# Gate and branch projections as seven half-size block products per column pair, gates ahead of branches

## The chip, the cores and the metric

The kernel is one inference step of a one-layer hybrid encoder and runs on one core of a Trainium2 chip. The metric is the device time of one launch in microseconds. Below, PE is TensorE (the matrix engine), DVE is VectorE, ACT is ScalarE, POOL is GpSimd and SP is the sync engine, whose queue issues the weight loads.

## The reference, cut to what matters

512 prompt tokens and 64 sample tokens (T = 576 together) pass through a mixer, a memory attention and a mixture of experts. The change is in the end of the mixer, which merges two branches under sigmoid gates:

```python
h = rmsnorm(x, norm_mix)                              # 576 x 1024
z, xbc_raw, dt_raw, q, k, v, gl_ssm, gl_sb = split_cols(h @ w_in)
...                                                   # y: the state-space scan, times d_skip and so on
y_ssm = rmsnorm(y * jax.nn.silu(z), ssm_norm) @ w_ssm_br            # K = 1024
y_sb = stick_breaking(qh, k_all, v_all, off).reshape(bsz, L, SB_INNER) @ w_sb_br   # K = 512
merged = jax.nn.sigmoid(gl_ssm) * y_ssm + jax.nn.sigmoid(gl_sb) * y_sb
return x + merged @ w_out, new_conv, h_last, kh, vh
```

Of this, three projections of 1024 x 1024 are touched: the two gate logits (`gl_ssm` and `gl_sb`, from `h`) and `y_ssm`. `y_sb`, with half their depth, is computed as before but at another time.

## The kernel before, in words

All activations lie transposed: 128 partitions of channels, 8 slices k, T = 576 token columns. A product is made exact to float32 by splitting each operand into a rounded high part and a low rest, and taking three matmuls, high x high, high x low and low x high (`passes`). `tproj` does this for one block of 128 output channels: two halves of 288 tokens, 8 slices, 3 matmuls, that is 48 matmuls of 128x288 (24 where the depth is 512). A weight tile comes in by SP (`load`) to one of four `RAW` buffers; ACT casts it to the high part (`split_high`), DVE subtracts to leave the rest in place (`split_low`).

The order of all work is written out by hand: each engine has its own program, and semaphores tie them. An engine executes strictly in its order, so what stands behind a waiting instruction waits too. The stages around the change are:

- the z projection (`z_rows(0..7)` on PE, `z_out` on ACT), with eight blocks of 128 channels;
- the state-space scan, ten steps v of `ssd_first` and `ssd_second` on PE, with exponentials on ACT, products on DVE (`xdt` and the lines behind it) and one product a step on POOL;
- the mixing stage, `for c in range(KD)` on each engine: for each of eight channel blocks c, PE makes both gate projections (48 matmuls each), the `w_ssm_br` projection (48) and the `w_sb_br` projection (24); ACT takes the sigmoids, DVE multiplies and adds (`mg_ready`), ACT and DVE split the result into `MGH` and `MG`. Weights of a block are two tiles, W_M + 2c and W_M + 2c + 1. Between the scan and the first branch product stand the squares of `ZS`, their sum over channels by PE (`squares_sum`) and `token_scale`, which is the rmsnorm factor `RB`;
- the output projection (`out_part`, `rproj`), which starts with the first seven slices of `MG`.

## Time and profile before

| | |
|---|---|
| median of 3 runs | 1194.85 us (1194.77 to 1195.83) |
| span of the profiled execution | 1192.3 us, so 2.55 us of the median lie around the span |
| PE, DVE, ACT, POOL busy | 1140.7, 715.9, 564.9, 121.0 us |
| mixing stage on PE | from 394.14 to 574.94 us, 180.8 us |

A busy PE counts each matmul until its modelled end, and the matmuls overlap; what one costs is therefore read from the starts of the first and the last of a run of them. DVE, ACT and POOL times are of the instructions themselves.

### The profile page before, as it was taken

Reading aid. Unit: us, or ns where it says so; the run is one execution under the profiler, and the core shown is the slowest. Engines: PE = TensorE matmul, PEld = TensorE weight load, DVE = VectorE, ACT = ScalarE, POOL = GpSimd, SP = SyncE. Lnnn points to the kernel's source line nnn. Section 1 sums busy time; section 2 is a strip of 40 time slices with the busy share of each in tenths; the row PEclk is TensorE's granted clock in tenths of the full one; section 3 lists DMA queues with packets and bytes.
Section 4 is the critical chain, followed back from the end, with each engine's and each line's share of the span. In section 5 each row is a group of like instructions: output and inputs, shape, how many; then the busy total and the mean of one; then the engine's idle time right before and its main releaser. Section 6 shows DMA issues by size and latency. Waiting matters only on the chain.

```text
span 1192.3 us, 18490 instructions
## 1 busy us (share of the span) xinstructions
PE 1140.7 (96%) x7908; PEld 1033.2 (87%) x7908; DVE 715.9 (60%) x850; ACT 564.9 (47%) x709; POOL 121.0 (10%) x147
## 2 busy tenths in 40 slices
PE   6999899999999999999999999999899999999994
PEld 6988789999986999999999999989667878778873
DVE  6325664866268642332535633534589998889884
ACT  6334553334386622222315523312176867778763
POOL 2003340000044000000000000000001000000050
PEclk9999989999999999999999999999799999999997
DMA  9421110323210232332526602201899999999995
GB/s 296 143 74 36 36 41 1 107 71 103 67 28 1 71 89 63 97 89 72 186 71 230 215 15 72 72 1 58 306 343 393 420 410 378 394 400 385 374 258 148
DMA packets 95038, 197.27 MB, mean 165 GB/s; under 512 B 4208, under 2 KB 71960, under 8 KB 82664
## 3 DMA queue, kind: packets, MB, share of 16 engines
q1 hardware_dynamic: 87328, 169.88, 40.5%
q0 software_dynamic: 5440, 18.76, 5.4%
q10 hardware_dynamic: 2184, 7.39, 1.5%
q8 instruction: 65, 1.06, 0.4%
q14 instruction: 21, 0.17, 0.1%
HBM read 178.41 MB, written 17.61 MB: 164 GB/s over the span
## 4 chain that ended last, share of the span: by engine, by line
PE 74%; DVE 10%; ACT 9%; issue 4%; DMA 2%; ACTq 0%; POOL 0%; SPq 0%; DVEq 0%; POOLq 0%
PE ps L2248 45%; PE ps L1032 6%; ACT buf_r L959 4%; DVE buf_r L966 4%; PE ps L1042 3%; PE ps L2688 2%; PE ps L2704 2%; PE ps L2369 1%; ACT buf_r L461 1%; DVE buf_r L1181 1%; PE ps L2398 1%; PE ps L2399 1%; PE ps L1016 1%; PE ps L2377 1%; ACT buf L1160 1%
## 5 line engine op out<-in xcount | busy, mean ns | idle before, releaser
L2248 PE MATMUL ps<-buf_r,buf_r 128*128 128x288 f32 (+1 forms) x4488 | 590.9, 292 | 7.3 <-ACT buf L1675 2.6
L2248 PEld LDWEIGHTS ps<-buf_r,buf_r 128*128 128x128 f32 x4488 | 578.8, 189 | 11.6 <-issue 6.7
L966 DVE TENSOR_TENSOR buf_r<-buf,buf_r 128x2048 fp32r<-128x2048 f32 x92 | 205.0, 2283 | 0.0
L1032 PE MATMUL ps<-buf_r,buf_r 128*128 128x512 f32 x720 | 174.5, 397 | 0.0
L959 ACT CAST buf_r<-buf 128x2048 fp32r<-128x2048 f32 x92 | 170.9, 1909 | 0.0
L446 DVE TENSOR_TENSOR buf_r<-buf,buf_r 128x2048 fp32r<-128x2048 f32 (+2 forms) x49 | 107.5, 2195 | 101.2 <-ACT buf_r L440 101.2
L1032 PEld LDWEIGHTS ps<-buf_r,buf_r 128*128 128x128 f32 x720 | 133.2, 188 | 29.7 <-issue 0.5
L440 ACT CAST buf_r<-buf 128x2048 fp32r<-128x2048 f32 (+2 forms) x53 | 96.7, 1824 | 99.6 <-PE ps L2248 55.1
L1042 PE MATMUL ps<-buf_r,buf_r 128*128 128x512 f32 x384 | 89.8, 389 | 0.5 <-DVE buf_r L1209 0.5
L1042 PEld LDWEIGHTS ps<-buf_r,buf_r 128*128 128x128 f32 x384 | 72.0, 188 | 15.8 <-DVE buf_r L1209 0.9
L461 ACT CAST buf_r<-ps 128x512 fp32r<-128x512 f32 (+2 forms) x41 | 30.0, 731 | 75.6 <-PE ps L1016 63.2
L558 ACT ACTIVATE buf<-buf 128x1024 f32<-128x1024 f32 (+1 forms) x22 | 23.2, 1056 | 43.0 <-DVE buf L2169 18.6
L1232 POOL DMA_INDIRECT buf<-hn_rows,buf x16 | 17.2, 1074 | 233.6 <-DVE buf L626 133.6
L1903 DVE COPY buf<-ps 128x1280 f32<-128x1280 f32 x10 | 14.9, 1490 | 36.1 <-PE ps L2369 29.7
L1565 POOL TENSOR_TENSOR buf<-buf,buf 128x1024 f32<-128x1024 f32 x10 | 27.8, 2783 | 58.1 <-ACT buf L1752 58.1
L1682 ACT ACTIVATE buf<-buf 128x1280 f32<-128x1280 f32 x10 | 12.7, 1275 | 41.4 <-POOL buf L1529 30.2
L1974 DVE SCALAR_TENSOR_TENSOR buf<-buf,buf,buf 128x579 f32<-128x579 f32 x36 | 29.6, 822 | 1.3
L1181 DVE TENSOR_TENSOR buf_r<-ps,buf_r 128x1024 fp32r<-128x1024 f32 x15 | 18.4, 1225 | 18.5 <-ACT buf_r L461 18.5
L461 ACT CAST buf_r<-buf 128x1024 fp32r<-128x1024 f32 (+4 forms) x20 | 19.0, 949 | 21.8 <-DVE buf L2105 11.6
L1817 ACT ACTIVATE buf<-ps 128x288 f32<-128x288 f32 x16 | 6.6, 411 | 46.5 <-PE ps L2248 46.5
L2398 PE MATMUL ps<-buf_r,buf_r 128*128 128x256 f32 (+1 forms) x78 | 26.8, 359 | 1.2 <-DVE buf_r L1913 1.2
L1529 POOL TENSOR_SCALAR_AFFINE_SELECT buf<-buf 128x128 f32<-128x128 f32 x32 | 20.2, 668 | 75.8 <-DVE buf L1903 75.8
(339 smaller groups left out, 1291.3 us busy)
## 6 DMA issues: line engine op xcount, KB each, us to landing
buf<-in_w_gate_e SPq DMA_DIRECT2D x32, 1024.0 KB, 8.1
buf<-in_w_up_e SPq DMA_DIRECT2D x32, 1024.0 KB, 7.6
buf<-in_w_down_e SPq DMA_DIRECT2D x32, 1024.0 KB, 7.4
buf<-in_w_in SPq DMA_DIRECT2D x16, 1024.0 KB, 5.6
buf<-in_w_in SPq DMA_DIRECT2D x17, 512.0 KB, 4.5
buf<-in_w_mem_kv SPq DMA_DIRECT2D x8, 1024.0 KB, 5.8
y_rows<-buf ACTq DMA_DIRECT2D x14, 512.0 KB, 8.4
buf<-in_x_prompt SPq DMA_DIRECT2D x8, 512.0 KB, 5.5
```

The costliest lines, as they stand in the source:

```text
L440: nc.scalar.copy(w_hi(n), tile_view(RAW[n % NRAW], n)).then_inc(wh_ready, 1)
L446: nc.vector.tensor_tensor(r32(raw), raw, w_hi(n), ALU.subtract).then_inc(wl_ready, 1)
L461: nc.scalar.copy(r32(hi), src).then_inc(ah_ready, 1)
L959: nc.scalar.copy(e_hi(t), e_raw(t)).then_inc(wh_ready, 1)
L966: nc.vector.tensor_tensor(e_lo(t), e_raw(t), e_hi(t), ALU.subtract).then_inc(wl_ready, 1)
L1032: last = nc.tensor.matmul(bank(b), r32(a[:, k, :]), w[:, i, :], start=(k == 0 and j == 0), stop=(k == KD - 1 and j == 2))
L1042: last = nc.tensor.matmul(bank(5 + c), r32(a[:, k, :]), w[:, i, 512 * c:512 * (c + 1)], start=(k == 0 and j == 0), stop=(k == 3 and j == 2))
L1181: nc.vector.tensor_tensor(r32(GT[e % 2]), bank(0, 2).rearrange("p (c n) -> p c n", c=KD), r32(GTH[e % 2]), ALU.subtract).then_inc(al_ready, 1)
L1565: nc.gpsimd.tensor_tensor(CE[v % 2], CE[v % 2], bc(XC[:, 10 + g, c * P:(c + 1) * P].unsqueeze(1), [P, 8, P]), ALU.mult).then_inc(ce_ready, 1)
L1974: o = nc.vector.scalar_tensor_tensor(out=cv[:, 0:579], in0=xr[:, j:j + 579], scalar=CW[:, j, i:i + 1], in1=cv[:, 0:579], op0=ALU.mult, op1 ...
L2248: last = nc.tensor.matmul(out, a, b, start=(k == 0 and j == 0), stop=(k == len(parts) - 1 and j == 2))
L2398: nc.tensor.matmul(out, m, high[:, oj:oj + nj], start=(j == kc), stop=False)
```

## The change

The eight blocks of each gate, and the eight of `w_ssm_br`, are now taken as column pairs i: i = 0 to 7 is block i of both gates, i = 8 to 11 is blocks 2(i - 8) and 2(i - 8) + 1 of `w_ssm_br`. For a pair, the weight is a 2 x 2 matrix of blocks (two column blocks by two halves of the depth), the activations are 2 x 2 as well (two halves of the depth by two halves of 288 tokens), and the eight block products are replaced by seven (the Winograd form of Strassen's scheme). That needs four sums of weight blocks for each pair (`sums`, in `S_RAW`), their high and low parts (`high_s`, `low_s`), four sums of activation blocks (T1 to T4) with high and low parts, made once for `h` and once for the scaled `ZS`, and copies and additions between the products (`u1_out`, `u2_out`, `u3_out` on ACT, `c11`, `c12`, `c22` on DVE). `MG` and `MGH` now hold the gates until the branch products meet them. `w_sb_br` is loaded in four chunks of two channel blocks into a buffer of its own (`SBR`, high part `SBH_`). The sums of squares and the scaling of the first gate by `RB` go to POOL. `MT` (memory tokens) is stored to a DRAM tensor early and loaded back behind the stage, since its place is needed.

The core of the diff:

```diff
+        m_tiles = []
         for c in range(0, D, P):
-            tiles.append(([(0, cols(w_in, C_GS + c, P)), (8, cols(w_in, C_GB + c, P))], P))
-            tiles.append(([(0, cols(I["w_ssm_br"][0], c, P)), (8, cols(I["w_sb_br"][0], c, P))], P))
+            m_tiles.append((cols(w_in, C_GS + c, P), cols(w_in, C_GB + c, P)))
+        for c in range(0, D, 2 * P):
+            m_tiles.append((cols(I["w_ssm_br"][0], c, P), cols(I["w_ssm_br"][0], c + P, P)))
...
+            return a[:, 4 * j:4 * j + 4, k * H2:(k + 1) * H2]
...
+        A_RAW = [RAW[i].rearrange("p (s n) -> p s n", n=P) for i in (1, 0)]
+        S_RAW = [RAW[i].rearrange("p (s n) -> p s n", n=P) for i in (2, 3)]
...
+            def load_m(i):
...
+                    sp.wait_ge(m_psum, m_at["p2", i - 2])
+                for j, src in enumerate(m_tiles[i]):
+                    sp.dma_start(A_RAW[i % 2][:, 8 * j:8 * j + 8, :], src).then_inc(ring_loaded[1 - i % 2], 16)
+            def load_sb(p):
+                if p == 0:
+                    sp.wait_ge(m_psum, m_at["p3", KD - 1])
+                else:
+                    sp.wait_ge(m_psum, m_at["sb", 2 * p - 1])
+                sp.dma_start(SBR, cols(I["w_sb_br"][0], 2 * P * p, 2 * P)).then_inc(mix_loaded, 16)
...
+            t_pool_step(1, T3, T3, r32(part(HT, 1, 1)), ALU.add)
+            t_pool_step(2, T3, T3, r32(part(HT, 0, 1)), ALU.subtract)
+            pool.wait_ge(t_made, 5)
+            t_pool_step(3, T4, r32(part(HTH, 1, 0)), T2, ALU.subtract)
+            t_pool_step(4, T4, T4, r32(part(HT, 1, 0)), ALU.add)
...
-            for c in range(KD):
...
-                nc.scalar.activation(halves(GS[c % 2]), pair(0), ACT.Sigmoid).then_inc(gs_ready, 1)
...
-                nc.scalar.activation(halves(GB[c % 2]), pair(2), ACT.Sigmoid).then_inc(gb_ready, 1)
-                split_high(act, W_M + 2 * c + 2)
...
+            def u3_out(i):
...
+                nc.scalar.copy(U3, x_sum(i)).then_inc(part_ready, 1)
...
+                act_high(MGH[:, c, :], MG[:, c, :])
+            def sb_high(p):
+                act.wait_ge(mix_loaded, 16 * (p + 1))
+                if p:
+                    act.wait_ge(m_psum, m_at["sb", 2 * p - 1])
+                nc.scalar.copy(r32(SBH_), SBR).then_inc(b_high, 1)
...
+            for i in range(NM):
+                u1_out(i)
+                if 1 <= i <= KD:
+                    gate_b_first(i - 1)
...
+                if i + 1 < NM:
+                    high_a(i + 1)
...
+                u2_out(i)
+                if i + 1 < NM:
+                    high_s(i + 1)
+                if 1 <= i <= KD:
...
+                    act_high(YSBTH, YSBT)
+                if i >= KD:
+                    sb_high(i - KD)
+                if i > KD:
+                    merged_high(2 * (i - KD - 1))
+                u3_out(i)
+                if i > KD:
+                    merged_high(2 * (i - KD - 1) + 1)
...
+                nc.vector.tensor_tensor(out, a, b, op).then_inc(t_made, 1)
...
+            dve.wait_ge(mt_stored, 16)
+            t_sum(0, T1, r32(part(HTH, 0, 1)), r32(part(HTH, 0, 0)), ALU.subtract)
+            t_sum(1, T1, T1, r32(part(HT, 0, 1)), ALU.add)
+            t_sum(2, T1, T1, r32(part(HT, 0, 0)), ALU.subtract)
+            t_sum(3, T2, r32(part(HTH, 1, 1)), T1, ALU.subtract)
+            t_sum(4, T2, T2, r32(part(HT, 1, 1)), ALU.add)
...
-            split_low(dve, W_M)
+            def sums(i):
...
+                nc.vector.tensor_tensor(o[:, 0:4], a[:, 8:12], a[:, 12:16], ALU.add).then_inc(sums_made, 1)
+                nc.vector.tensor_tensor(o[:, 8:12], a[:, 0:4], a[:, 8:12], ALU.subtract)
+                dve.wait_ge(sums_made, 3 * i + 1)
+                nc.vector.tensor_tensor(o[:, 4:8], o[:, 0:4], a[:, 0:4], ALU.subtract).then_inc(sums_made, 1)
+                dve.wait_ge(sums_made, 3 * i + 2)
+                nc.vector.tensor_tensor(o[:, 12:16], a[:, 4:8], o[:, 4:8], ALU.subtract).then_inc(sums_made, 1)
...
+            def low_a(i):
...
+                nc.vector.tensor_tensor(r32(A_LOW[q]), A_RAW[q][:, 12:16], r32(A_HIGH[q][:, 8:12]), ALU.subtract)
+                nc.vector.tensor_tensor(r32(A_RAW[q][:, 0:8]), A_RAW[q][:, 0:8], r32(A_HIGH[q][:, 0:8]),
+                                        ALU.subtract).then_inc(m_low, 1)
+            def low_s(i):
...
+                dve.wait_ge(m_high, 2 * i + 2)
+                nc.vector.tensor_tensor(r32(S_RAW[i % 2]), S_RAW[i % 2], r32(S_HIGH[i % 2]), ALU.subtract).then_inc(m_low, 1)
...
+            def t_rest(count, low, raw, high):
...
+                dve.wait_ge(b_high, count)
+                nc.vector.tensor_tensor(r32(low), raw, r32(high), ALU.subtract).then_inc(b_low, 1)
+            sums(0)
+            dve.wait_ge(t_pool, 5)
+            t_rest(T_G["T1"], T1, T1, T1H)
+            t_rest(T_G["T2"], T2, T2, T2H)
+            low_a(0)
...
+            def c22(i):
+                dve.wait_ge(part_ready, 3 * i + 3)
+                dve.wait_ge(m_psum, m_at["p5", i])
...
+                nc.vector.tensor_tensor(out, z_sum(i), U3, ALU.add).then_inc(block_done, 1)
...
+            def merge(c):
+                dve.wait_ge(m_psum, m_at["sb", c])
+                dve.wait_ge(gate_ready, 2 * c + 2)
...
+                nc.vector.tensor_tensor(gb, pair(6), gb, ALU.mult).then_inc(mg_ready, 1)
+                dve.wait_ge(mg_ready, 2 * c + 1)
+                dve.wait_ge(m1_done, 2 * (c // 2 + 1))
+                nc.vector.tensor_tensor(MG[:, c, :], MGH[:, c, :], M1[c % 2], ALU.add).then_inc(mg_ready, 1)
...
+            def sb_low(p):
+                dve.wait_ge(b_high, len(T_G) + len(T_Z) + p + 1)
+                nc.vector.tensor_tensor(r32(SBR), SBR, r32(SBH_), ALU.subtract).then_inc(b_low, 1)
...
-                act_low(dve, A_MG + c + 1, MG[:, c, :], MGH[:, c, :])
+                    c22(i - 1)
+                if i > KD:
+                    branch_b(i - 1 - KD)
+                if i == KD:
+                    dve.wait_ge(m_psum, m_at["p7", KD - 1])
+                    t_sum(0, T3, part(ZS, 1, 1), part(ZS, 0, 1), ALU.subtract)
+                    dve.wait_ge(t_made, 8)
+                    t_sum(0, part(ZS, 0, 1), part(ZS, 1, 0), T2, ALU.subtract)
+                    t_rest(T_Z["T2"], T2, T2, T2H)
+                    z_rest("B21", 1, 0)
+                if i >= 1:
+                    c12(i - 1)
+                if i > KD:
+                    branch_a(i - 1 - KD)
+                if i + 1 < NM:
+                    sums(i + 1)
+                if i == 0:
+                    t_rest(T_G["T3"], T3, T3, T3H)
+                    dve.wait_ge(so_psum, 2)
+                if i + 1 < NM:
+                    low_a(i + 1)
...
+                if i == KD - 1:
+                    dve.wait_ge(sq_ready, 2 * KD)
+                    dve.wait_ge(m_psum, m_at["p5", KD - 1])
+                    t_sum(0, T1, part(ZS, 0, 1), part(ZS, 0, 0), ALU.subtract)
+                    z_rest("B11", 0, 0)
+                    dve.wait_ge(m_psum, m_at["p6", KD - 1])
+                    dve.wait_ge(t_made, 6)
+                    t_sum(0, T2, part(ZS, 1, 1), T1, ALU.subtract)
+                if i == KD:
+                    t_rest(T_Z["T3"], T3, T3, T3H)
+                if i > KD:
+                    merge(2 * (i - KD - 1))
+                c11(i)
+                if i == KD - 1:
+                    t_rest(T_Z["T1"], T1, T1, T1H)
+                if i + 1 < NM:
+                    low_s(i + 1)
+                if i == KD:
+                    z_rest("T4", 0, 1)
+                    z_rest("B22", 1, 1)
+                    act_low(dve, A_YSB + 1, YSBT, YSBTH)
+                if i >= KD:
+                    sb_low(i - KD)
+                if i > KD:
+                    merged_low(2 * (i - KD - 1))
+                    merge(2 * (i - KD - 1) + 1)
+                    merged_low(2 * (i - KD - 1) + 1)
+            c22(NM - 1)
...
+            def product(out, a_hi, a_lo, b_hi, b_lo, first):
+                for k in range(4):
+                    for j, (a, b) in enumerate(((a_hi, b_hi), (a_hi, b_lo), (a_lo, b_hi))):
+                        last = nc.tensor.matmul(out, r32(a[:, k, :]), r32(b[:, k, :]), start=(first and k == 0 and j == 0),
+                                                stop=(k == 3 and j == 2), skip_group_check=not first)
...
+            def p3(i):
+                pe.wait_ge(b_low, first_with(i, "B22"))
+                pe.wait_ge(block_done, c_at(22, i))
+                product(z_sum(i), S_HIGH[i % 2][:, 12:16], S_RAW[i % 2][:, 12:16], part(HTH, 1, 1), part(rest(i), 1, 1),
+                        False).then_inc(m_psum, 1)
+            def p4(i):
+                pe.wait_ge(b_low, first_with(i, "T4"))
+                pe.wait_ge(part_ready, 3 * i + 3)
+                product(x_sum(i), A_HIGH[i % 2][:, 8:12], A_LOW[i % 2], part(HTH, 0, 1), part(rest(i), 0, 1),
+                        False).then_inc(m_psum, 1)
...
+            for i in range(NM + 1):
+                if i < NM:
+                    p1(i)
+                if i >= 1:
+                    p4(i - 1)
+                    p3(i - 1)
+                if i > KD:
+                    sb(2 * (i - KD - 1))
+                if i < NM:
+                    p5(i)
+                    p6(i)
+                    p2(i)
+                    p7(i)
+                if i == 4:
                     squares_sum()
-                    pe.wait_ge(al_ready, A_ZS + KD)
-                    tproj(4, nb, 0, ZSH, ZS).then_inc(br_psum, 1)
+                if i > KD:
+                    sb(2 * (i - KD - 1) + 1)
             st_m = lambda flat, k, m: r32(flat[:, k * T + m * P:k * T + m * P + P])
```

PE's loop gives this order: p1(i), p4(i-1), p3(i-1), then sb of an even block where i > 8, then p5(i), p6(i), p2(i), p7(i), and then sb of the odd block where i > 8. Each p is 12 matmuls of 128x288, each sb is 24.

Three places of the order are shown. On DVE before, an end of one block and the start of the next (L2099, L2102 and L2105 merge, L446 is a weight's rest, L2093 scales the gate):

```order
L2099 TENSOR_TENSOR buf_163<-ps,buf_152 128x576 [waits gs_scaled,br_psum]
L2102 TENSOR_TENSOR buf_150<-ps,buf_154 128x576 [waits gb_ready,sb_psum]
L2105 TENSOR_TENSOR buf_150<-buf_150,buf_163 128x576 [waits m2_done,m1_done]
L446 TENSOR_TENSOR buf_66_r<-buf_66,buf_70_r 128x1536 [waits wh_ready]
L465 TENSOR_TENSOR buf_150_r<-buf_150,buf_161_r 128x576 [waits ah_ready]
L2093 TENSOR_TENSOR buf_153<-buf_153,buf_156 128x576 [waits gs_ready]
L446 TENSOR_TENSOR buf_67_r<-buf_67,buf_71_r 128x2048 [waits wh_ready]
```

After, where the gates end and the branches begin (iterations i = 7 and 8; buf_127 is ZS, buf_95, buf_97 and buf_162 are T1, T2 and T3, L2268 is `t_sum`, L2327 is `t_rest`, L2410 is `c22(7)`):

```order
L2268 TENSOR_TENSOR buf_95<-buf_127 128x1152 [waits m_psum,sq_ready]
L2327 TENSOR_TENSOR buf_127_r<-buf_127,buf_50_r 128x4x288 [waits b_high]
L2268 TENSOR_TENSOR buf_97<-buf_127,buf_95 128x1152 [waits t_made,m_psum]
L2392 TENSOR_TENSOR buf_165<-ps,buf_53 128x288 [waits m_psum,part_ready]
L2327 TENSOR_TENSOR buf_95_r<-buf_95,buf_96_r 128x1152 [waits b_high]
L2322 TENSOR_TENSOR buf_71_r<-buf_71,buf_85_r 128x2048 [waits m_high]
L2410 TENSOR_TENSOR buf_169<-ps,buf_100 128x288 [waits out_stored,m_psum,part_ready]
L2268 TENSOR_TENSOR buf_162<-buf_127 128x1152 [waits m_psum]
L2268 TENSOR_TENSOR buf_127<-buf_127,buf_97 128x4x288 [waits t_made]
L2327 TENSOR_TENSOR buf_97_r<-buf_97,buf_98_r 128x1152 [waits b_high]
L2327 TENSOR_TENSOR buf_127_r<-buf_127,buf_50_r 128x4x288 [waits b_high]
L2398 TENSOR_TENSOR buf_165<-ps,buf_173 128x288 [waits m_psum,part_ready]
```

Eight instructions of 1152 columns (128x4x288 is that too) have come in between these; behind the rows shown, in iteration 8, follow three more (the rests of T3, T4 and of a quarter of ZS), the rest of `YSBT` (2304 columns) and that of the first `w_sb_br` chunk (1024), all ahead of `c22(8)`.

On SP, at the start of the branches (buf_175 is `SBR`; buf_70 and buf_69 are the two weight buffers). Before, each `w_sb_br` block went with its `w_ssm_br` block in one of four ring buffers; now it waits for `m_psum`, that is for the last product that reads the chunk before it:

```order
L1563 DMA buf_175<-in_w_sb_br 128x4x256 [waits m_psum]
L1556 DMA buf_70<-in_w_ssm_br 128x8x128 [waits m_psum]
L1556 DMA buf_70<-in_w_ssm_br 128x8x128
L1563 DMA buf_175<-in_w_sb_br 128x4x256 [waits m_psum]
L1556 DMA buf_69<-in_w_ssm_br 128x8x128 [waits m_psum]
L1556 DMA buf_69<-in_w_ssm_br 128x8x128
L1563 DMA buf_175<-in_w_sb_br 128x4x256 [waits m_psum]
L1520 DMA buf_70<-in_w_out 128x8x256 [waits zt_psum,m_psum]
L1520 DMA buf_71<-in_w_out 128x8x256 [waits zt_psum,m_psum]
L1563 DMA buf_175<-in_w_sb_br 128x4x256 [waits m_psum]
```

On ACT, iteration i = 9 (L1989 is `sb_high(1)`, L503 is `merged_high`, L1960 is `u3_out(9)`, L1948 is `u1_out`, L1868 `high_a`, L1876 `high_s`):

```order
L1948 COPY buf_53<-ps 128x288 [waits block_done,m_psum]
L1868 CAST buf_86_r<-buf_70 128x1024 [waits m_psum,ring_loaded1]
L1869 CAST buf_86_r<-buf_70 128x512
L1954 COPY buf_173<-ps 128x288 [waits block_done,m_psum]
L1876 CAST buf_85_r<-buf_71 128x2048 [waits m_psum,sums_made]
L1989 CAST buf_176_r<-buf_175 128x1024 [waits m_psum,mix_loaded]
L503 CAST buf_169_r<-buf_165 128x576 [waits mg_ready]
L1960 COPY buf_100<-ps 128x288 [waits block_done,m_psum]
L503 CAST buf_169_r<-buf_165 128x576 [waits mg_ready]
L1948 COPY buf_53<-ps 128x288 [waits block_done,m_psum]
```

The cast of the `w_sb_br` chunk stands ahead of the copy U3 in ACT's order. In the old loop ACT had, for one block:

```order
L1783 ACTIVATE buf_153<-ps 128x576 [waits gs_psum]
L1787 ACTIVATE buf_155<-ps 128x576 [waits gb_psum]
L440 CAST buf_71_r<-buf_67 128x2048 [waits ring_loaded1,gb_psum]
L440 CAST buf_70_r<-buf_68 128x1536 [waits ring_loaded2,sb_psum]
L461 CAST buf_161_r<-buf_150 128x576 [waits mg_ready]
```

## Rows read from the trace of the kernel before

**Rows 1.** The page: head, engines (busy, share), chain that ended last

```profile
span 1192.3 us, 18490 instructions
...
PE 1140.7 (96%) x7908; PEld 1033.2 (87%) x7908; DVE 715.9 (60%) x850; ACT 564.9 (47%) x709; POOL 121.0 (10%) x147
...
PE 74%; DVE 10%; ACT 9%; issue 4%; DMA 2%; ACTq 0%; POOL 0%; SPq 0%; DVEq 0%; POOLq 0%
```

**Rows 2.** Busy time by stretch: scan, stage's start, rest of the stage

```profile
core 0: us, PE busy (x) PEld busy (x) DVE busy (x) ACT busy (x) POOL busy (x), PEclk, DMA share, GB/s
327.00:394.00 67.00, 63.72 (x639) 50.50 (x638) 51.00 (x82) 49.85 (x109) 27.83 (x10) 1.00 0.05 13
394.00:419.00 25.00, 23.87 (x177) 23.16 (x176) 17.97 (x23) 19.89 (x25) 1.88 (x2) 1.00 0.31 85
419.00:574.00 155.00, 155.00 (x1169) 155.00 (x1170) 54.00 (x50) 36.78 (x36) 0.00 (x0) 1.00 0.34 95
```

**Rows 3.** Timeline of PE, start and us: the mixing stage and what follows

```profile
394.14 16.15 PE L2248 MATMUL ps<-buf_r,buf_r 128*128 128x288 f32 x120
...
418.85 61.39 PE L2248 MATMUL ps<-buf_r,buf_r 128*128 128x288 f32 x461 [1.13 <-DVE buf_r L446]
...
574.94 5.91 PE L2611 MATMUL ps<-buf_r,buf_r 128*128 128x256 f32 x48
```

**Rows 4.** Groups by shape, 419 to 574 us: busy, mean ns

```profile
L446 DVE TENSOR_TENSOR buf_r<-buf,buf_r 128x2048 fp32r<-128x2048 f32 x7 | 16.0, 2292 | 51.9 <-ACT buf_r L440 51.9
L440 ACT CAST buf_r<-buf 128x2048 fp32r<-128x2048 f32 x7 | 13.3, 1897 | 0.0
L446 DVE TENSOR_TENSOR buf_r<-buf,buf_r 128x1536 fp32r<-128x1536 f32 x7 | 12.3, 1751 | 0.0
L440 ACT CAST buf_r<-buf 128x1536 fp32r<-128x1536 f32 x7 | 10.3, 1478 | 44.5 <-PE ps L2248 44.5
...
L465 DVE TENSOR_TENSOR buf_r<-buf,buf_r 128x576 fp32r<-128x576 f32 x7 | 5.3, 752 | 0.0
L461 ACT CAST buf_r<-buf 128x576 fp32r<-128x576 f32 x7 | 4.7, 674 | 2.9 <-DVE buf L2105 2.9
```

**Rows 5.** Timeline of ACT and of DVE: the stage's start

```profile
391.42 2.12 ACT L461 CAST buf_r<-buf 128x2304 fp32r<-128x2304 f32 x1 [4.95 <-PE ps L2555]
...
411.77 1.28 ACT L1775 ACT_TABLE_LOAD   x1
...
395.56 2.55 DVE L465 TENSOR_TENSOR buf_r<-buf,buf_r 128x2304 fp32r<-128x2304 f32 x1
```

**Rows 6.** Timeline of ACT and PE where the scan starts

```profile
326.59 0.71 ACT L1734 ACTIVATE buf<-ps 128x288 f32<-128x288 f32 x2 [3.88 <-PE ps L2248]
327.32 1.28 ACT L1752 ACT_TABLE_LOAD   x1
...
334.24 0.71 ACT L1734 ACTIVATE buf<-ps 128x288 f32<-128x288 f32 x2
...
335.26 0.38 PE L2543 MATMUL ps<-buf 128*128 128x512 bf16 x1
```

**Rows 7.** Timeline of DVE, POOL and PE, scan steps 4 and 5

```profile
361.16 2.34 DVE L446 TENSOR_TENSOR buf_r<-buf,buf_r 128x1536 fp32r<-128x1536 f32 x1
...
365.40 2.60 DVE L2054 TENSOR_TENSOR buf<-buf,buf 128x1024 f32<-128x1024 f32 x1
...
369.52 0.67 DVE L2065 TENSOR_TENSOR buf<-buf,ps 128x512 f32<-128x512 f32 x1
...
358.89 2.99 POOL L1565 TENSOR_TENSOR buf<-buf,buf 128x1024 f32<-128x1024 f32 x1 [2.60 <-ACT buf L1752]
364.47 2.45 POOL L1565 TENSOR_TENSOR buf<-buf,buf 128x1024 f32<-128x1024 f32 x1 [2.59 <-ACT buf L1752]
...
370.92 0.38 PE L2543 MATMUL ps<-buf 128*128 128x512 bf16 x1
```

**Rows 8.** DMA issues, 400 to 560 us: KB each, median us to landing

```profile
buf<-in_w_in SPq DMA_DIRECT2D x12, 512.0 KB, 4.8
buf<-in_w_ssm_br SPq DMA_DIRECT2D x6, 512.0 KB, 4.1
```

**Rows 9.** PE near the program's start, and the granted clock (eighth column, PEclk)

```profile
14.68 1.76 PE L2303 MATMUL ps<-buf_r,buf_r 128*128 128x256 f32 x8 [3.30 <-ACT buf_r L461]
...
14.00:16.00 2.00, 1.32 (x7) 1.35 (x8) 1.43 (x2) 1.54 (x3) 0.00 (x0) 0.76 1.08 336
16.00:18.00 2.00, 2.00 (x12) 2.00 (x11) 1.59 (x2) 1.68 (x6) 0.00 (x0) 0.50 1.09 394
18.00:20.00 2.00, 2.00 (x17) 1.92 (x16) 1.23 (x1) 1.56 (x5) 0.00 (x0) 0.89 1.01 379
```

494 lines of the change are left out of this document (370 added, 124 removed).

## The prediction, made before the changed kernel ran

> **What bounds the kernel now.** I read the page first: PE is busy 96% of the span and the chain that ended last lies 74% on it [rows 1]. Then busy time by stretch: from 419 to 574 us PE has 155.00 of 155.00 us, DVE 54.00 and ACT 36.78, at granted clock 1.00 [rows 2]. The mixing stage is bound by PE alone, so a matmul taken out there is worth its full pitch. The timeline gives it: from 418.85 to the output projection at 574.94 stand seven blocks of 168 matmuls, 156.09 / 1176 = 0.1327 us each [rows 3]. A product of 12 is 1.59 us. The whole stage lasts 180.8 us, 1344 matmuls (178.4), the sum of squares and one idle of 1.13 us [rows 3].
>
> **What is removed.** Twelve pairs with seven products for eight: 12 x 12 = 144 matmuls, **-19.1 us**. The idle of 1.13 us, with its order of casts, goes too: **-1.1**.
>
> **What the added work costs on DVE and ACT.** On DVE 2304 columns take 2.55 us and 576 take 0.75 [rows 4, 5], so 1.04 ns a column and 0.15 fixed, of which the next instruction hides about 0.08. The pitch is then 0.37 us for 288 columns, 0.60 for 512, 1.14 for 1024, 1.27 for 1152, 2.2 for 2048. On ACT 2304 take 2.12 and 576 take 0.67 [rows 4, 5]: 0.4 for 288, 1.1 for 1152, 1.5 for 1536, 1.9 for 2048. I add 0.1 for each hand-over between engines. A gate pair takes PE 7 x 1.59 = 11.15 us; DVE needs 2.5 (`sums`) + 1.7 (`low_a`) + 2.2 (`low_s`) + 1.1 (three additions) = 7.5, ACT 1.5 + 1.9 + 1.2 + 1.4 (gates) = 6. So the gate pairs stay bound by PE, if the order lets them. I therefore followed the order of waits, product by product, and found five places where PE stands.
>
> (a) **Before the scan, +1.8.** `T1H` and `T2H`, 2 x 1.1 us, are cast right behind `z_out(6)` (326.59), ahead of the scan's first exponential. That moves ACT's `z_out(7)` from 334.24 to 336.4, ending at 337.1; PE's first second half, which started at 335.26 [rows 6], waits for it.
>
> (b) **In the scan, +1.1.** At steps 4 and 5 DVE gets 0.53 (2048 for 1536 columns) and 1.27 (rest of T4). PE starts at 370.92 what DVE's instruction of 369.52 (0.67) had freed at 370.2 [rows 7]: 0.7 us are covered, 1.1 are not. POOL's five sums lie beside the z projection, ACT's other casts in its idle time of the steps.
>
> (c) **Pairs 0 to 6, +3.4.** In pairs 0 to 3 ACT has two squares and two scalings (0.6 each) ahead of `u2_out`, and the second square waits for POOL's addition; `p7` then starts 0.5 us late in most of them: 2.0. In pair 5 `token_scale` brings a table load, and the sigmoids another (1.28 [rows 5]) ahead of `u3_out(5)`, which ends 14.1 us after the pair's start while `p4(5)` could start at 12.8: 1.4 with its hand-over.
>
> (d) **From gates to branches, +13.6.** Between the end of `p3(6)` and `p3(8)` DVE has, without a gap: six additions (2.2), two `sums` (5.0), two `low_a` (3.5), two `low_s` (4.4), eleven instructions of 1152 columns (14.0), the rest of `YSBT` (2.5) and of the first chunk (1.1): 32.7 us, with 0.1 to PE 32.8. PE has 13 products in between, 20.7. The difference, 12.1, is waited in pieces before `p3(7)`, `p7(8)`, `p4(8)` and `p3(8)`. POOL scales two gates in this stretch. DVE's 1536 columns took 2.34 us where they take 1.75, and 1024 took 2.60 for 1.22, both while POOL's instruction ran [rows 4, 7]; two of POOL's of 576 columns, 1.4 us each by its 2.45 for 1024, may cost DVE 0 to 2.8; I take 1.5.
>
> The Trainium skill ("SBUF — State Buffer", Who interferes with whom) says that POOL and a DVE instruction with two SBUF inputs exclude each other for the whole instruction. The rows agree: the 2.60 us instruction of 365.40 ended 1.1 us after POOL's end at 366.92 [rows 7]. By that rule the term would be 2.8 in place of 1.5, and the prediction 1.3 us more.
>
> (e) **The chunks of `w_sb_br`, 3 x 7.65 and 2.5 more, +25.5.** `SBR` has one buffer, so chunk p is loaded only when sb(2p-1) has ended on PE. But ACT's `sb_high(p)` stands ahead of `u3_out(i)`, i = 8 + p, without which `p4(i)` cannot start, and `p4(i)` is only one product behind sb(2p-1). From the end of sb(2p-1) = 0: the load lands at 4.6 (512 KB took 4.1 and 4.8 [rows 8]), ACT casts until 5.6, then `merged_high` 6.2 and U3 6.6, so `p4(i)` starts at 6.7 and not at 1.6. DVE takes the rest of the chunk (6.8), `merged_low` (7.5), `merge` (8.95), the next `merged_low` behind ACT (10.4), and only then `c22(i)` (10.8). `p3(i)` runs from 10.85 to 12.45 and not to 4.8: 7.65 lost, for p = 1, 2 and 3. Behind the third, DVE has `c12`, `branch_a`, the rest of W_O (to 15.8) and only then the product of `merge(6)`, for which sb(7) waits: it ends at 19.8, where PE alone would be through at 9.6. That is 10.2, 2.55 over the 7.65.
>
> (f) **The clock, +5.1.** After 3.30 us of idle the granted clock was 0.76, 0.50 and 0.89 in the next three stretches of 2 us [rows 9], so 1.7 us of full speed were lost. PE's wait of 5.1 us before each of `p4(9)`, `p4(10)`, `p4(11)` is longer; I count 1.7 for each. It may be 0 (no fall), or double, since PE waits again 2.5 us later and once 4 us before `p7(8)`.
>
> Behind the stage I count nothing: the residual rows and W_O's second half are loaded 7 us before the output projection, `MT` has some 50 us, and its splits fall in idle time of ACT and DVE.
>
> The sum: -19.1 - 1.1 + 1.8 + 1.1 + 3.4 + 13.6 + 25.5 + 5.1 = +30.3 us on a span of 1192.3 [rows 1], 1222.6; with the 2.55 us that lie around it before, **1225 us**. Its own range is 1212 (no clock term, landings at the short end, no lock, (c) hidden) to 1240 (clock doubled, lock whole, casts and additions meeting each other's queues).
>
> **The rivals.** *PE stays the bound, faster.* DVE is idle 101 of 155 us and ACT 118 [rows 2], so if the five steps of waits were covered in (d), (e) and (f), there would remain, of (e), 0.6 a pair for DVE's longer list and 1.4 at the end: 1194.85 - 19.1 - 1.1 + 2.9 + 3.4 + 3.2 = 1184. The other terms sum to -13.9, so the sign turns when (d), (e) and (f) together cost less than 13.9 us, where I have 44.2. Against it: idle time is before or behind the stretch of (d), not in it, and the chunk's load alone (4.1) with its cast (0.95) is longer than the one product of 1.6 before `p4(i)`.
>
> *Only the chunks are covered* (their load not what is waited for): 1184 + 13.6 = 1198. It needs a copy landed within a microsecond; the shortest row says 4.1.
>
> *Only the hand-over is covered*, with (e) and (f) as they are: 1184.2 - 3.2 + 25.5 + 5.1 = 1212. It needs DVE's 32.7 us to be 12 less; the rows leave 1 to 2.
>
> *Worse than forecast*, above 1240: the clock stays down through the branch pairs (four times 17.5 us of PE at half speed would be up to 70 more), or a table load appears in each pair. PE's busy stretches of 8 us and more between the waits speak against the first.
>
> **How the numbers follow.** The forecast holds 0.81, only the hand-over covered 0.05, only the chunks covered 0.04, PE still the bound 0.05, worse 0.05. The predicted time is the forecast's. The range of 1207 to 1241 takes in its own range and the third rival's 1212, and leaves out 0.14 of these and a little of the forecast. A change of 0.2% (2.4 us) is about what a measurement of this kernel can tell from none; 1198 is 3 us above the time before, so some of it counts as the same. Faster 0.05, same 0.03, slower 0.92.
>
> **What the new profile would show.** PE has 1200 matmuls of 128x288 in the stage and its first starts near 397. Up to pair 6 a pair takes 11 to 12 us. Then four waits, for DVE and once for ACT, between `p3(7)` and `p3(8)`, 12 to 14 us in sum. Then, three times, a wait of about 5 us for ACT's U3 copy, itself behind the cast of `in_w_sb_br`'s chunk, which waits for its DMA; and one of 2 to 3 us for DVE. The output projection starts near 605. The clock falls at the three long waits. I am wrong if the chunk's cast waits for nothing, if DVE has gaps between pair 7 and `p3(8)`, or if PE's waits sum to less than 19 us.

## The result, and the profile of the changed kernel

The changed kernel takes **1224.45 us** (median of 4 runs, 1222.39 to 1226.94) beside 1194.81 us before (4 runs): ratio 1.0246, 95% interval 1.0219 to 1.0273. 1225 us was forecast. The profiled execution spans 1220.7 us.

The page of the changed kernel: its head, its engines, the chain that ended last and the group of the block products, to be set against [rows 1]:

```profile
span 1220.7 us, 18593 instructions
...
PE 1136.3 (93%) x7764; PEld 1024.9 (84%) x7764; DVE 816.0 (67%) x957; ACT 606.0 (50%) x787; POOL 166.9 (14%) x168
...
PE 67%; DVE 14%; ACT 10%; issue 5%; DMA 4%; ACTq 0%; POOL 0%; SPq 0%; DVEq 0%; POOLq 0%
...
L2982 PE MATMUL ps<-buf_r,buf_r 128*128 128x288 f32 x1008 | 150.7, 311 | 31.1 <-ACT buf L1960 13.8
```

PE has its 144 matmuls fewer (7764 for 7908), yet its busy time fell by only 4.4 us, since some of the rest ran at half clock; its share of the chain fell from 74% to 67%, and the seven block products (L2982) have 31.1 us of idle time in front of them, 13.8 of it, the largest part, for ACT's U3 copy (L1960). DVE gained 100 us of work.

The timeline of PE through the mixing stage, which from 418.85 on was one gapless block before [rows 3]; a new row begins where PE waited (the value in brackets) or where the line changes, L2982 being the p products and L2646 sb:

```profile
398.59 6.64 PE L2982 MATMUL ps<-buf_r,buf_r 128*128 128x288 f32 x48
405.62 4.98 PE L2982 MATMUL ps<-buf_r,buf_r 128*128 128x288 f32 x36 [0.39 <-ACT buf L1954]
...
432.58 9.80 PE L2982 MATMUL ps<-buf_r,buf_r 128*128 128x288 f32 x72 [1.08 <-DVE buf_r L2316]
...
494.33 4.95 PE L2982 MATMUL ps<-buf_r,buf_r 128*128 128x288 f32 x24 [2.50 <-issue]
499.84 3.42 PE L2982 MATMUL ps<-buf_r,buf_r 128*128 128x288 f32 x24 [0.57 <-DVE buf L2410]
503.68 3.44 PE L2982 MATMUL ps<-buf_r,buf_r 128*128 128x288 f32 x24 [0.41 <-DVE buf_r L2327]
511.02 7.30 PE L2982 MATMUL ps<-buf_r,buf_r 128*128 128x288 f32 x36 [3.91 <-DVE buf_r L2327]
521.05 1.82 PE L2982 MATMUL ps<-buf_r,buf_r 128*128 128x288 f32 x12 [2.73 <-DVE buf L2410]
522.72 3.34 PE L2646 MATMUL ps<-buf_r,buf_r 128*128 128x288 f32 x24
...
532.24 3.33 PE L2646 MATMUL ps<-buf_r,buf_r 128*128 128x288 f32 x24
535.40 1.75 PE L2982 MATMUL ps<-buf_r,buf_r 128*128 128x288 f32 x12
541.31 3.22 PE L2982 MATMUL ps<-buf_r,buf_r 128*128 128x288 f32 x12 [4.16 <-ACT buf L1960]
545.69 3.22 PE L2982 MATMUL ps<-buf_r,buf_r 128*128 128x288 f32 x12 [1.16 <-DVE buf L2410]
548.71 4.04 PE L2646 MATMUL ps<-buf_r,buf_r 128*128 128x288 f32 x24
...
558.96 3.33 PE L2646 MATMUL ps<-buf_r,buf_r 128*128 128x288 f32 x24
...
608.57 5.92 PE L3078 MATMUL ps<-buf_r,buf_r 128*128 128x256 f32 x48
```

The wait of 2.50 us that the profile puts to nothing (`issue`) ends 0.1 us after DVE has finished an L2327, the rest of a quarter of `ZS` (491.66 to 494.22), which p1(8) needs.

The stage lasts 210.0 us, and 180.8 before. From sb(1) at 532.24 to sb(3) at 558.96, one branch pair, are 26.7 us where its 132 matmuls need 17.5. Why p4(9) started only at 541.31 is told by the other engines' timelines, SP's queue, ACT and DVE:

```profile
535.59 0.37 SPq L1563 DMA_DIRECT2D buf<-in_w_sb_br  x1
...
539.25 1.04 ACT L1989 CAST buf_r<-buf 128x1024 fp32r<-128x1024 f32 x1 [7.77 <-DMA buf<-in_w_sb_br]
540.20 0.67 ACT L503 CAST buf_r<-buf 128x576 fp32r<-128x576 f32 x1
540.77 0.39 ACT L1960 COPY buf<-ps 128x288 f32<-128x288 f32 x1
...
540.33 1.23 DVE L2440 TENSOR_TENSOR buf_r<-buf,buf_r 128x1024 fp32r<-128x1024 f32 x1 [6.52 <-ACT buf_r L1989]
...
545.10 0.45 DVE L2410 TENSOR_TENSOR buf<-ps,buf 128x288 f32<-128x288 f32 x1
```

The chunk is issued as sb(1) ends and lands 3.6 us later; behind its cast on ACT stand a merged block's cast and then U3. On DVE the chunk's rest, a merged block's rest, a merge and the next block's rest (0.74 us of waiting for ACT among them) stand ahead of c22 (L2410). The granted clock in the same stretch (PEclk, eighth column):

```profile
539.00:541.00 2.00, 0.00 (x0) 0.00 (x0) 0.67 (x1) 1.75 (x3) 0.00 (x0) 0.75 1.13 299
541.00:543.00 2.00, 1.69 (x7) 1.72 (x8) 1.97 (x4) 0.17 (x1) 0.00 (x0) 0.50 0.61 154
...
547.00:549.00 2.00, 2.00 (x10) 2.00 (x10) 0.00 (x0) 0.00 (x0) 0.00 (x0) 0.50 0.00 0
...
551.00:553.00 2.00, 2.00 (x18) 2.00 (x17) 1.88 (x4) 0.00 (x0) 0.00 (x0) 1.00 0.00 0
```

It fell to 0.50 (1.2 of 2.4 GHz) towards the end of the wait and stayed there for some 9 us: p4(9) took 3.22 us for 1.75, p3(9) the same, sb(2) 0.7 more than its twin.

### The profile page after: what moved, and what is told of

The parts are those of the page before. It is cut to its first block, busy times and chain, and to the rows that moved or that the text cites. A ratio compares the mean times of both kernels' runs of the same rounds, so it can differ in the third digit from the quotient of the medians.

```text
span 1220.7 us, 18593 instructions
## 1 busy us (share of the span) xinstructions
PE 1136.3 (93%) x7764; PEld 1024.9 (84%) x7764; DVE 816.0 (67%) x957; ACT 606.0 (50%) x787; POOL 166.9 (14%) x168
## 4 chain that ended last, share of the span: by engine, by line
PE 67%; DVE 14%; ACT 10%; issue 5%; DMA 4%; ACTq 0%; POOL 0%; SPq 0%; DVEq 0%; POOLq 0%
PE ps L2646 33%; PE ps L2982 7%; PE ps L1100 6%; DVE buf_r L1034 4%; ACT buf_r L1027 4%; PE ps L1110 3%; PE ps L3156 1%; PE ps L3172 1%; ACT buf_r L503 1%; PE ps L2767 1%; DMA buf<-in_w_in 1%; DVE buf_r L1249 1%; PE ps L2796 1%; PE ps L2797 1%; DVE buf_r L2322 1%
## 5 line engine op out<-in xcount | busy, mean ns | idle before, releaser
L2646 PE MATMUL ps<-buf_r,buf_r 128*128 128x288 f32 (+1 forms) x3336 | 440.2, 291 | 7.4 <-ACT buf L1804 2.6
L2646 PEld LDWEIGHTS ps<-buf_r,buf_r 128*128 128x128 f32 x3336 | 428.1, 190 | 11.7 <-issue 8.1
L1034 DVE TENSOR_TENSOR buf_r<-buf,buf_r 128x2048 fp32r<-128x2048 f32 x92 | 205.1, 2283 | 0.0
L2982 PE MATMUL ps<-buf_r,buf_r 128*128 128x288 f32 x1008 | 150.7, 311 | 31.1 <-ACT buf L1960 13.8
L2982 PEld LDWEIGHTS ps<-buf_r,buf_r 128*128 128x128 f32 x1008 | 144.8, 201 | 35.8 <-issue 25.7
L488 DVE TENSOR_TENSOR buf_r<-buf,buf_r 128x2048 fp32r<-128x2048 f32 (+1 forms) x33 | 75.8, 2300 | 39.2 <-ACT buf_r L482 39.2
L482 ACT CAST buf_r<-buf 128x2048 fp32r<-128x2048 f32 (+1 forms) x37 | 69.6, 1882 | 54.1 <-PE ps L2670 40.0
L503 ACT CAST buf_r<-ps 128x512 fp32r<-128x512 f32 (+2 forms) x41 | 30.0, 731 | 75.9 <-PE ps L1084 63.6
L1300 POOL DMA_INDIRECT buf<-hn_rows,buf x16 | 17.5, 1096 | 233.5 <-DVE buf L694 133.5
L2148 DVE COPY buf<-ps 128x1280 f32<-128x1280 f32 x10 | 14.9, 1490 | 35.8 <-PE ps L2767 29.8
L2322 DVE TENSOR_TENSOR buf_r<-buf,buf_r 128x2048 fp32r<-128x2048 f32 x12 | 30.4, 2535 | 1.8 <-ACT buf_r L1876 1.5
L503 ACT CAST buf_r<-buf 128x1024 fp32r<-128x1024 f32 (+4 forms) x20 | 18.9, 947 | 23.5 <-DVE buf L2433 17.7
```

The lines of the kernel that those rows point to most:

```text
L482: nc.scalar.copy(w_hi(n), tile_view(RAW[n % NRAW], n)).then_inc(wh_ready, 1)
L488: nc.vector.tensor_tensor(r32(raw), raw, w_hi(n), ALU.subtract).then_inc(wl_ready, 1)
L503: nc.scalar.copy(r32(hi), src).then_inc(ah_ready, 1)
L1034: nc.vector.tensor_tensor(e_lo(t), e_raw(t), e_hi(t), ALU.subtract).then_inc(wl_ready, 1)
L2322: nc.vector.tensor_tensor(r32(S_RAW[i % 2]), S_RAW[i % 2], r32(S_HIGH[i % 2]), ALU.subtract).then_inc(m_low, 1)
L2646: last = nc.tensor.matmul(out, a, b, start=(k == 0 and j == 0), stop=(k == len(parts) - 1 and j == 2))
```

## Where the time went, stretch by stretch

Each value is a difference of two PE starts in a profile's timeline, in us. "Scan" is from the first float32 matmul of its first second half (336.20 us in the changed kernel) to the first gate product; "pairs" to the product behind the wait of 2.50 (in e9_pool 1.30); "hand-over" from there to sb(0); "branches" to the output projection. "Stage" is the sum of the three. PE alone would need 87.0 for the pairs (54 products and the sum of squares), 15.9 for the hand-over (10 products) and 57.3 for the branches (20 products, eight sb). The last column is from the output projection to the end of the span.

| kernel | scan | pairs | hand-over | branches | stage | behind | median |
|---|---|---|---|---|---|---|---|
| before | 58.7 | | | | 180.8 | 617.4 | 1194.8 |
| changed | 62.4 | 95.7 | 28.4 | 85.9 | 210.0 | 612.1 | 1224.45 |
| e1_order | 62.4 | 95.8 | 28.4 | 77.5 | 201.7 | 610.6 | 1217.0 |
| e5_order2 | 62.4 | 95.7 | 29.1 | 65.3 | 190.1 | 613.7 | 1205.5 |
| e12_buffer | 62.4 | 96.3 | 29.8 | 66.8 | 192.9 | 611.7 | 1207.1 |
| e2_chunks | 62.4 | 95.8 | 29.2 | 66.8 | 191.9 | 612.3 | 1207.3 |
| e6_chunks2 | 62.4 | 97.0 | 29.4 | 60.0 | 186.4 | 612.4 | 1201.0 |
| e3_hand | 62.4 | 95.6 | 25.8 | 83.8 | 205.3 | 612.9 | 1219.9 |
| e4_scan | 57.6 | 95.8 | 28.4 | 85.7 | 209.9 | 613.7 | 1220.6 |
| e11_casts | 62.4 | 95.8 | 29.5 | 85.9 | 211.2 | 613.3 | 1224.7 |
| e8_squares | 62.4 | 108.7 | 28.4 | 83.6 | 220.6 | 612.5 | 1241.9 |
| e9_pool | 62.4 | 90.4 | 27.5 | 83.7 | 201.7 | 613.4 | 1215.8 |
| e7_best | 57.7 | 95.8 | 25.9 | 59.3 | 181.1 | 613.6 | 1190.5 |
| e10_more | 57.6 | 92.3 | 24.8 | 60.3 | 177.4 | 613.8 | 1186.2 |

What lies ahead of the scan moves by up to 5 us from one profile to the next, in work that no kernel changed, so the stretches tell more than the spans. A profile is of one execution, and not of the median one: that of the changed kernel is 2.1 us below its median, that of e1_order 4.0 and that of e8_squares 6.6 below, that of e3_hand 3.4 above.

## The experiments

### The chunks of w_sb_br: order or buffer

`e1_order` moves two calls. (Here and below, lines in a diff that name an engine list its calls in their order, cut to those that matter.)

```diff
 ACT, iteration i > KD
-    sb_high(i - KD); merged_high(2q); u3_out(i); merged_high(2q + 1)
+    merged_high(2q); u3_out(i); sb_high(i - KD); merged_high(2q + 1)
 DVE
-    low_s(i + 1); sb_low(i - KD); merged_low(2q)
+    c22(i - 1); branch_b; sb_low(i - 1 - KD); c12(i - 1)
```

(q = i - 9.) Expected:

> The changed kernel with its two lists re-ordered in the branch pairs alone: ScalarE casts chunk p of w_sb_br behind its copy of U3, and VectorE takes the chunk's rest behind c22 and branch_b in the next iteration. The chunk's buffer stays single and is loaded as late as before. Theory (the wait is made by the order, because U3 and c22 stand behind a cast that waits for its transfer): from the end of sb(2p-1) the chunk lands at 3.7 us, is cast by 4.8, its rest is there at 6.1; p4 and p3 no longer wait, sb(2p) starts at 6.2 where its operands allow 4.8. So 1.4 us a pair are lost and some 3 at the tail, where it was 28.6 in all: 1224.5 - 21 = 1203 us (1200 to 1207), and the granted clock no longer falls in the branch pairs. Rival 1 (the transfer itself is the wait, whatever the order): under 6 us won, 1219 or more. Rival 2 (VectorE's list in these pairs is the bound): under 6 us won, and VectorE shows no gaps there.

Measured: 1217.0 us (1212.96 to 1222.05), ratio 1.0200 (1.0172 to 1.0227). The branches won 8.4 us, not 21. The second rival does not hold, since DVE has gaps of 3.7 us; the first had 1219 or more, inside the spread of these runs, and only the next run settles it. ACT, DVE and PE of this kernel:

```profile
539.60 1.04 ACT L1989 CAST buf_r<-buf 128x1024 fp32r<-128x1024 f32 x1 [6.33 <-DMA buf<-in_w_sb_br]
540.55 0.67 ACT L503 CAST buf_r<-buf 128x576 fp32r<-128x576 f32 x1
541.25 0.76 DVE L507 TENSOR_TENSOR buf_r<-buf,buf_r 128x576 fp32r<-128x576 f32 x1 [3.67 <-ACT buf_r L503]
541.93 0.45 DVE L2412 TENSOR_TENSOR buf<-ps,buf 128x288 f32<-128x288 f32 x1
...
542.52 2.34 PE L2987 MATMUL ps<-buf_r,buf_r 128*128 128x288 f32 x12 [3.33 <-DVE buf L2412]
```

U3 is free, but c22 (L2412) still waits for the chunk by a detour: `merged_low` (L507) ahead of it waits for `merged_high`, which now stands behind the chunk's cast. The edit had moved the wait from p4 to p3. `e5_order2` takes that link out:

```diff
 ACT
-    sb_high(i - KD); merged_high(2q + 1)
+    merged_high(2q + 1); sb_high(i - KD)
 DVE
-    merge(2q + 1); merged_low(2q + 1); c22(i); branch_b
+    merge(2q + 1); c22(i); branch_b; merged_low(2q + 1)
```

> The re-ordered kernel mended where its trace showed the wait to have gone: on ScalarE the cast of merged_high(2q+1) now stands ahead of the chunk's cast, and on VectorE merged_low(2q+1) stands behind c22 and branch_b. The chunk's buffer stays single. Theory (the first re-ordering fell short, 8.3 us of the stage won for 21, because c22 still stood behind merged_low, this behind merged_high, and this behind the chunk's cast on ScalarE): p3(9), p3(10) and p3(11) no longer wait (3.3, 3.4 and 4.8 us), sb(2), sb(4) and sb(6) wait 1.4 us each for the chunk, and some 3 us of granted clock come back: stage 201.7 - 10.8 = 191 us, whole 1206 us (1204 to 1208). Rival (the single buffer's load is what is waited for, whatever stands where): within 2 us of the first re-ordering, 1215 or more.

Measured: 1205.5 us (ratio 1.0096, 1.0075 to 1.0117), stage 190.1 for the 191 expected. PE:

```profile
538.88 4.95 PE L2988 MATMUL ps<-buf_r,buf_r 128*128 128x288 f32 x36
545.23 3.43 PE L2652 MATMUL ps<-buf_r,buf_r 128*128 128x288 f32 x24 [1.40 <-DVE buf_r L2441]
```

p1, p4 and p3 run without a gap, sb(2) waits 1.40 us for the chunk's rest, and no clock is lost behind it. The first rival of e1_order is out with that. So 20.5 of the 28.5 us that the branches lose were order alone, with the same late load into the same single buffer; by the medians the kernel is 18.9 us faster.

`e12_buffer` keeps the order of the changed kernel and takes two buffers of half the size:

```diff
-    SBR, SBH_ = A.view(4, 2 * P), A.view(4, 2 * P)
+    SBR, SBH_ = ([A.view(4, P) for _ in range(2)] for _ in range(2))
-    chunk p loaded behind sb(2p - 1)
+    column c loaded behind sb(c - 2)
```

> Single-column chunks of w_sb_br in two buffers, but in the order of the changed kernel: ScalarE casts the even chunk ahead of merged_high and U3, VectorE takes its rest ahead of merged_low and so ahead of c22. Theory (order and buffer are two cures of one wait: a cast that stands ahead of U3 costs only its 0.6 us when its chunk has long landed): the same as with both, stage 192 us, whole 1207 us (1205 to 1209). Rival (the order is needed too): 1213 or more, with waits of 3 us before p4.

Measured: 1207.1 us (ratio 1.0107, 1.0091 to 1.0124), branches 66.8: the order is not needed too. `e2_chunks` has the buffer and, of the first re-ordering, ACT's part. On DVE its edit moves the even column's rest only behind `merged_low(2q)`, still ahead of c22, which is less than its expectation says:

> As the kernel with the two lists re-ordered, and the chunks of w_sb_br are single columns of 128 in two buffers each (the same memory), so that a chunk is loaded one whole pair ahead. Theory (what is left after the re-ordering is the load behind sb(2p-1)): all of the 28.6 us of the branch pairs go but about 3 for VectorE's longer list and the tail: 1198 us (1196 to 1201), 4 to 6 us below the re-ordered kernel. Rival 1 (the order was all): the same as the re-ordered kernel within 1 us. Rival 2 (twice as many transfers of half the row length land late): above the re-ordered kernel.

Measured: 1207.3 us (ratio 1.0104, 1.0084 to 1.0124) and branches 66.8 again: beside the buffer ACT's re-ordering gives nothing. I had expected 1198, because I took all remaining waits for the load's. They were again of order: sb(3) waited 2.05 us because DVE took the odd column's rest only behind `low_s`. `e6_chunks2` re-orders four such places (c22 and branch_b ahead of `merged_low`, the odd column's rest ahead of c11, W_O's first piece one pair earlier on ACT and on DVE):

> The kernel with single-column chunks in two buffers, with four places mended: c22 and branch_b ahead of merged_low(2q+1); the rest of the odd chunk ahead of c11; W_O's first piece cast and its rest taken one pair earlier. Theory (its remaining waits in the branch pairs, 0.41, 0.43 and 2.03 us before p3, 2.05 before sb(3), 1.27 before sb(7), are all of order): stage 191.9 - 6.2 = 185.7 us, whole 1201 us (1200 to 1202.5). Rival (VectorE's total work in a branch pair is the bound): under 2 us won, 1205 or more, and VectorE without gaps there.

Measured: 1201.0 us (ratio 1.0065, 1.0042 to 1.0087). The branches take 60.0 us, 2.7 above PE's own, and p1, p4 and p3 of pairs 9 and 10 run without a wait. What is left is 0.8 us before p3(11), 0.9 before sb(7) and the clock at sb(0).

### The hand-over

`e3_hand`:

```diff
 DVE, iteration 8
-    low_s(9); rest of T4; rest of B22; rest of YSBT; sb_low(0)   [iteration 9] c22(8); branch_b(0)
+    rest of T4; rest of B22; c22(8); rest of YSBT; sb_low(0)     [iteration 9] branch_b(0); low_s(9)
```

> The changed kernel with three VectorE instructions moved in the hand-over from gates to branches: c22(8) stands ahead of the rests of YSBT and of the first chunk, and low_s(9) behind c22(8) and branch_b(0). Nothing else changes. Theory (between pair 7 and sb(0) VectorE works without a gap and is the bound, so what p3(8) and sb(0) do not need may be taken out ahead of them): low_s(9), 2.3 to 3.1 us, and the overlap of the two rests with p3(8), 1.6 us: 1224.5 - 4.7 = 1219.8 us (1218 to 1221.5). Rival (TensorE's waits there are for something else, a cast of ScalarE or its own queue): no change, within 1 us.

Measured: 1219.9 us (ratio 1.0205, 1.0188 to 1.0223), stage 4.7 us shorter. PE:

```profile
515.70 8.52 PE L2985 MATMUL ps<-buf_r,buf_r 128*128 128x288 f32 x48 [3.90 <-DVE buf_r L2327]
524.81 3.44 PE L2649 MATMUL ps<-buf_r,buf_r 128*128 128x288 f32 x24 [0.59 <-DVE buf_r L2440]
```

p7(8), p1(9), p4(8) and p3(8) are one piece now; the wait ahead of p7(8) stays. The hand-over itself is 2.6 us shorter, not 4.7: the four products take 8.52 us, and 6.4 at full clock, which DVE's work no longer hides. The other 2.1 us are in the branches, where after a wait of 4.0 us before p4(9) the clock was back for p3(9) (1.82 us for 3.22). That was in no theory, so the agreement with 4.7 is in part luck. DVE's list is the bound here: in the trace of the changed kernel it has no gap from 485.57 to 521.6, and the three moves shorten the hand-over.

### GpSimd beside VectorE

`e9_pool` lets the fifteen POOL instructions of this stage work on 8 of 576 columns:

```diff
-    nc.gpsimd.tensor_tensor(RB, RB, SQT, ALU.add)
+    nc.gpsimd.tensor_tensor(RB[:, 0:8], RB[:, 0:8], SQT[:, 0:8], ALU.add)
-    nc.gpsimd.tensor_tensor(MG[:, c, :], MG[:, c, :], RB, ALU.mult)
+    nc.gpsimd.tensor_tensor(MG[:, c, 0:8], MG[:, c, 0:8], RB[:, 0:8], ALU.mult)
```

> The changed kernel with GpSimd's seven additions of squares and eight scalings of gates working on 8 columns where they work on 576: the scale per token and the scaled gates come out wrong for the rest, and the time is read for the lock alone. Theory (a GpSimd instruction and a VectorE instruction with two SBUF inputs keep each other out, so these fifteen lengthen VectorE's in pairs 1 to 3, 1.83 and 1.94 us for 0.69, and in the hand-over, 2.56 for 1.34 and 3.14 for 2.28): the waits of 1.1 us before p1 in two pairs and the 2.1 us in the hand-over go: 1224.5 - 4.5 = 1220 us (1218.5 to 1221.5). Rival (VectorE's own work is what is waited for, the lock falls into its idle time): no change within 1 us.

Measured: 1215.8 us (ratio 1.0177, 1.0161 to 1.0192), 8.7 us less, nearly twice what I expected. 5.3 of it are in the pairs, 0.9 in the hand-over, 2.1 in the branches, where the clock again came back before p3(9) (1.83 us), after a wait of 4.30. Instructions of `sums` and of the rest behind them on DVE and POOL's addition, changed kernel:

```profile
415.04 1.87 DVE L2306 TENSOR_TENSOR buf<-buf,buf 128x512 f32<-128x512 f32 x1
...
417.61 2.44 DVE L2316 TENSOR_TENSOR buf_r<-buf,buf_r 128x1024 fp32r<-128x1024 f32 x1
...
414.91 1.45 POOL L1694 TENSOR_TENSOR buf<-buf,buf 128x576 f32<-128x576 f32 x1 [6.77 <-ACT buf L1933]
417.21 1.75 POOL L1694 TENSOR_TENSOR buf<-buf,buf 128x576 f32<-128x576 f32 x1 [0.86 <-ACT buf L1933]
```

and the same two DVE instructions without POOL's:

```profile
415.56 0.69 DVE L2306 TENSOR_TENSOR buf<-buf,buf 128x512 f32<-128x512 f32 x1
...
416.95 1.22 DVE L2316 TENSOR_TENSOR buf_r<-buf,buf_r 128x1024 fp32r<-128x1024 f32 x1
```

Each grew by 1.2 us beside a POOL instruction of 1.45 to 1.75, and with them the rest that p1 of the next pair needs. Here PE was late itself; one pair on, where L2302 and L2306 of the changed kernel took 1.94 and 1.82 us for 0.69, p1 waited the 1.08 us of the row at 432.58. The Trainium skill ("SBUF — State Buffer", Who interferes with whom) states exclusion for the whole instruction, and these rows agree. The two of DVE end 0.55 and 1.09 us behind POOL's, near their own 0.69 and 1.22.

The edit does not test that exclusion alone. In the changed kernel ACT's second square waits 0.81, 0.85 and 1.30 us for POOL's addition in pairs 1 to 3, which needs no exclusion, and in e9_pool it waits for nothing. So 1.0 of the 5.3 us, before p7, may be the shorter addition itself.

`e8_squares` met the same exclusion from the other side. It moves the two squares of pairs 0 to 3:

```diff
 ACT, iteration i < 4
-    high_a(i + 1); square(2i); square(2i + 1); u2_out(i); high_s(i + 1); gates(i - 1)
+    high_a(i + 1); u2_out(i); high_s(i + 1); square(2i); square(2i + 1); gates(i - 1)
```

> The changed kernel with the squares of pairs 0 to 3 placed behind high_s on ScalarE, and not ahead of u2_out. Theory (p7 of pairs 0 and 1 waits for u2_out, which stands behind two squares and two scalings): the waits of 0.66 and 1.2 us before these p7 go: 1224.5 - 1.8 = 1222.7 us, and the gates' stretch from the first gate product to the end of p7(7), 93.2 us, becomes 91.4. Rival (ScalarE's total work per pair is what is waited for, so high_s or U3 is late instead): no change within 0.7 us, and the waits stand before p4.

Measured: 1241.9 us (ratio 1.0412, 1.0389 to 1.0434), 17 us slower. POOL, ACT and PE:

```profile
420.44 2.92 POOL L1694 TENSOR_TENSOR buf<-buf,buf 128x576 f32<-128x576 f32 x1 [9.10 <-ACT buf L1933]
...
423.45 0.68 ACT L1933 ACTIVATE buf<-buf 128x576 f32<-128x576 f32 x1 [2.28 <-POOL buf L1694]
...
425.75 0.38 ACT L1960 COPY buf<-ps 128x288 f32<-128x288 f32 x1
...
426.27 12.75 PE L2982 MATMUL ps<-buf_r,buf_r 128*128 128x288 f32 x84 [3.97 <-ACT buf L1960]
```

The squares now fall beside DVE's `low_s` of 2048 columns, so POOL's addition takes 2.92 us for 1.45 (low_s ran from 419.81 to 422.10, and the addition ended 1.3 us after it); the second square waits for it, U3 stands behind the square, and p4 waits 3.97 us in three pairs. My rival had the place right; neither theory had its size, nor the clock that went with it.

### The scan and what precedes it

`e4_scan` puts `low_s(0)` at step 9 (from 4), the rest of T4 at step 8 (from 5), and T3H's cast behind the scan.

> The changed kernel with low_s(0) at the scan's step 9 and the rest of T4 at step 8, where they stood at steps 4 and 5; the cast of T3H, which needs the rest of T4, stands behind the scan. Theory (the two instructions of 2048 and 1152 columns delay VectorE there, and put its 1024-column product of the next step beside a POOL instruction, 2.91 us for 1.22): of the 3.7 us that the scan lost, most come back, since VectorE has idle time of 1.0 and 2.0 us in the last two steps: 1224.5 - 2.5 = 1222 us (1221 to 1223). The first gate product starts 2 to 3 us earlier. Rival (they cost as much at any step): no change, within 0.7 us; the last steps then show the same waits.

Measured: 1220.6 us (ratio 1.0208, 1.0191 to 1.0225), scan 57.6 us for 62.4: 4.8 won, more than the 3.7 the change had cost, since before too a rest of 1536 columns stood at step 4 [rows 7]. DVE and POOL of the changed kernel, from step 4 on, show where most of it was:

```profile
361.88 2.87 DVE L2322 TENSOR_TENSOR buf_r<-buf,buf_r 128x2048 fp32r<-128x2048 f32 x1
...
365.27 2.81 DVE L2374 TENSOR_TENSOR buf<-buf,buf 128x512 f32<-128x512 f32 x1
...
375.13 2.91 DVE L2358 TENSOR_TENSOR buf<-buf,buf 128x1024 f32<-128x1024 f32 x1
...
365.19 2.35 POOL L1685 TENSOR_TENSOR buf<-buf,buf 128x1024 f32<-128x1024 f32 x1 [2.59 <-ACT buf L1907]
...
374.59 2.37 POOL L1685 TENSOR_TENSOR buf<-buf,buf 128x1024 f32<-128x1024 f32 x1 [7.05 <-ACT buf L1907]
```

Behind the longer rest (L2322) the state product L2374 starts just as POOL's instruction of the next step does, and takes 2.81 us for 0.68; two steps later the 1024 columns of L2358 take 2.91 for 1.22. Both end 0.5 to 1.1 us after POOL's end (367.54 and 376.96), as if they had begun there. Before, the rest of 1536 columns and one instruction behind it met POOL so, 2.34 us for 1.75 and 2.60 for 1.22 [rows 7]. So a delayed DVE pays a second time. An instruction with a PSUM input does not: in the kernel before, this one ran inside POOL's 364.47 to 366.92 in its usual time:

```profile
364.80 0.69 DVE L2072 TENSOR_TENSOR buf<-buf,ps 128x512 f32<-128x512 f32 x1
```

`e11_casts` puts T1H's and T2H's casts behind `z_out(5)`:

> The changed kernel with the casts of T1H and T2H behind z_out(5) in place of z_out(6), where ScalarE is idle for 4.2 us; nothing else moves. Theory (2.2 us of casts delay the scan's first exponential, and with it z_out(7) and TensorE's first second half): 1224.5 - 1.9 = 1222.6 us, and from the end of the z projection's step 0 to the scan's first second half 2 us less. Rival (the delay is one of the table loads, or of VectorE's rests): no change within 0.7 us.

Measured: 1224.7 us, no change in the whole (1221.36 to 1226.31). Yet the stretch ahead of the scan, from PE's last matmuls of its step 0 to the first second half, is 9.90 us in the changed kernel, 8.08 in this one and 8.10 before. The 1.8 us are there; in this execution the stage was 1.3 us longer (sb and p at half clock again), and four runs that spread over 5 us don't show the remainder. By the time alone the rival, no change, stands; the stretch speaks for the theory.

### All together

`e7_best` is e6, e3 and e4 in one kernel.

> All mended orders together: single-column chunks in two buffers with the four places mended, the three VectorE instructions moved in the hand-over, and low_s(0) and the rest of T4 at the scan's last two steps. If the causes found are separate, their gains add: 1224.5 - 18.1 - 6.2 - 4.7 - 4.8 = 1190.7 us, 0.35% below the kernel before (1189.5 to 1192.5). Rival (they overlap, since what the hand-over gives is waited again before sb(0) or p5(9)): 1194 to 1197, the same as before. Left of the change's costs in either case: some 10 us of VectorE's work between pair 7 and p3(8), some 5 in pairs 0 to 6, 1.8 ahead of the scan.

Measured: **1190.5 us** (12 runs), ratio 0.9974 (0.9959 to 0.9990). The stage is 181.1 us; taking the single gains as measured, 23.6 (e6), 4.7 (e3) and 0.1 (e4), off 210.0 gives 181.6. They add. (By the medians the single gains, 23.4, 4.5 and 3.9, would give 1192.6 us.) `e10_more` adds e11's casts and takes the squares' additions from POOL to DVE:

```diff
-    (POOL) nc.gpsimd.tensor_tensor(RB, RB, SQT, ALU.add).then_inc(sq_sum, 1)
+    (DVE)  nc.vector.tensor_tensor(RB, RB, (SQT, MG[:, KD - 1, :])[k % 2], ALU.add).then_inc(sq_sum, 1)
```

> The kernel of all mended orders (1190.5 us) with two edits more: the additions of squares stand on VectorE, with MG's last column as a second buffer, so GpSimd runs beside no sums of pairs 0 to 3; and T1H and T2H are cast one column block of z earlier, in ScalarE's idle time of 4 us. Theory: 2.7 us of waits before p1 go, 1.8 ahead of the scan: 1186 us (1184.5 to 1187.5), 0.7% below the kernel before. Rival (VectorE is full in pairs 0 to 3 and 0.75 us more for each square delays c11 and low_s): 1189 to 1191.

Measured: **1186.2 us** (6 runs), ratio 0.9934 (0.9919 to 0.9949). Pairs 92.3 for 95.8: seven additions of 0.75 on a DVE that has room cost less than seven of 1.45 on a POOL that keeps it waiting. The stretch ahead of the scan is 8.08 us again, as in e11_casts.

## Why the prediction was right, term by term

The direction, the place and the mechanism of the loss were right, and so was each large term to within 2 us or so. That the time is 0.6 us from the forecast is luck, since errors cancel: forecast +30.3 on the span, measured +28.4, of which +34.7 in the stretches that the terms are about, -5.3 behind them and -1.1 ahead.

- **Removed, -19.1 and -1.1**: right. There are 144 matmuls fewer, and at 0.1327 us a matmul the terms add up to the stage within 0.3 us: 180.8 - 19.1 - 1.1 + 6.2 + 15.0 + 28.5 = 210.3.
- **(a) +1.8**: measured 9.90 - 8.10 = 1.8.
- **(b) +1.1 was mis-sized, +3.7**: DVE's two added pieces were costed as their own length less a cover of 0.7. The step that failed is the cover: they also shift what follows them beside POOL's instruction, where two of DVE's grew by 2.1 and 1.7 us. The effect stands in [rows 7], and I had used it only for (d).
- **(c) +3.4, measured 6.2**: waits of 0.2 to 1.1 us before p7, p3 and p1. Taking what PE loses by the starts of its rows, what I listed was about right: 2.4 us before p7 for ACT (2.0 forecast) and 0.9 in pair 5 (1.4). What the sum lacked is DVE's lengthened work beside POOL's additions, 2.6 us before p3(0), p1(3) and p1(4). Without POOL's work (e9_pool) 4.1 of the 6.2 are gone: these 2.6, 1.0 of the 2.4, 0.4 of the 0.9 and 0.1 of the rest. (The stretch is 5.3 shorter; 1.2 of it is the wait at 494, which belongs to (d).)
- **(d) +13.6, measured 15.0** (491.83 to 522.72 is 30.9, less ten products of 1.59): DVE without a gap, as forecast. The places of the waits were less exact: one of 2.50 us stands before p1(8), which I had not listed, and none before p4(8). PE ran below full clock here too (7.30 us for 36 matmuls that need 4.8), which costs next to nothing while DVE is the bound. The two lengthened instructions here (2.56 for 1.34 at 491.66, 3.14 for 2.28 at 511.25) are 2.1 us, between my 1.5 and the 2.8 of full exclusion.
- **(e) +25.5 and (f) +5.1, together 30.6, measured 28.5**: the mechanism is shown by e5 and by e12, each of which takes it away in its own manner. Its parts were off in opposite directions: the clock cost 3.7, 4.0 and 1.7 us in pairs 9, 10 and 11, 9.4 for the 5.1 of (f), and the waits 19.1 for the 25.5 of (e). For pair 9 the waits are 4.3 and 1.2 us (541.31 less 537.0, and 545.69 less the half-speed product), 5.5 for the 7.65 forecast, since the chunk landed in 3.6 us and not 4.6 and p4 at half speed hid some of c22's lateness; the clock is 1.6 + 1.4 + 0.7 = 3.7 for the 1.7 forecast.
- **"Behind the stage I count nothing"**: wrong by 5.3 us in the two profiles. Until 1157.9 us before (1191.8 after) the changed kernel keeps 33.9 us behind, at the end 28.4. PE's last product group on the timeline, before and then after:

```profile
1169.62 1.65 PE L894 MATMUL ps<-buf_r,buf_r 128*128 128x512 f32 x3 [2.86 <-DVE buf_r L1175]
1174.57 8.94 PE L894 MATMUL ps<-buf_r,buf_r 128*128 128x512 f32 x29 [3.30 <-issue]
```

```profile
1202.78 7.62 PE L962 MATMUL ps<-buf_r,buf_r 128*128 128x512 f32 x32 [2.11 <-DVE buf_r L1243]
```

Before, PE stopped for 3.30 us after three matmuls, for nothing that the profile shows, and then ran below full clock; in none of the thirteen later kernels of the table is the part behind the stage longer than 613.8 us. No second profile of the kernel before exists, and no experiment was made on the stop, so its cause stays open. The medians speak for the code and against that one execution: the edited stretches account for +34.7 (changed), +1.1 (e7_best) and -4.5 us (e10_more) against before, the medians for +29.6, -3.8 and -8.3, so 4 to 5 us of each lie elsewhere. The rest, 1.1 us in the other direction ahead of the stage, is inside what the profiles vary by.

The rivals: "only the chunks covered" was priced at 1198 and "PE stays bound" at 1184. The kernel with the chunks covered came to 1201. The best one came to 1186, yet PE is not its bound throughout: its stage is 177.4 us where PE alone needs 160.2, so it is near 1184 for other reasons: its scan and the stretch ahead of it lost nothing, where the rival has 2.9 us of cost and the runs a gain of 1.1, and 3.8 us lie elsewhere, as above. The removed matmuls took off their 19 us; what the change put around them cost 55 (3.7 + 1.8 + 6.2 + 15.0 + 28.5), and the stage of the best order is 3.4 us shorter than before.

## What to carry to other kernels

Where a load into a single buffer is late, look first at what stands behind its first user on each engine: moving a few calls out from behind it won 19 us (1224.5 to 1205.5) with the load as late as ever, and the detour over a second engine's list (a cast behind the cast, a rest behind that) has to be cut too, or the wait only changes its product. When work is taken off the bound engine and given to the others, add up the helper's whole list between two deadlines, at the joints of the loop above all, and not per iteration. And cost an added VectorE instruction by the GpSimd instruction that it, or its successor, will meet.

## What the runs showed of the hardware

- GpSimd and VectorE kept each other out in both directions: DVE instructions with two SBUF inputs took 1.8 to 2.9 us where they take 0.7 to 1.2, and a POOL addition took 2.92 for 1.45 beside DVE's 2048 columns. An instruction of DVE with a PSUM input kept its 0.69 inside a POOL instruction (364.80, before).
- The granted clock fell to 0.50 with PE's waits of 4.2 to 5.5 us before p4(9), p4(10) and p4(11) and cost 3.7, 4.0 and 1.7 us in the changed kernel. After a like wait before p4(9) it cost only 1.6 in e9_pool (4.30 us of wait) and 1.5 in e3_hand (4.04), since it was back for p3(9). After the waits of 1.3 to 1.7 us in e5_order2 it did not fall. A wait of 2.05 us before sb(3) was followed by a fall in e12_buffer and by full clock in e2_chunks, and the 2.50 before p1(8) likewise by a fall in the changed kernel (4.95 us for 24 matmuls) and by full clock in e7_best (3.42): one length of wait, both outcomes, and what decides is left open. The rows of sb(3), e12_buffer and then e2_chunks:

```profile
556.53 4.97 PE L2661 MATMUL ps<-buf_r,buf_r 128*128 128x288 f32 x24 [2.05 <-DVE buf_r L2450]
...
557.62 3.43 PE L2663 MATMUL ps<-buf_r,buf_r 128*128 128x288 f32 x24 [2.05 <-DVE buf_r L2452]
```

- 512 KB of `w_sb_br` in rows of 1 KB landed in 3.6 us (median of 4, 3.4 to 4.4), below the 4.1 of [rows 8]. For the second chunk no load was under way when it was issued; the next two were issued 0.4 us behind it.
